# Projection units 3 to 8 of a decoder layer by seven block products

## What is computed

```
proj = x @ w_in                      # x (1032, 1024), w_in (1024, 2568)
u_pool, q, k, v, o_pre, gates = split(proj)      # 512 each, gates 8
y_pool = pool mixer of u_pool;  h = mLSTM(q, k, v, gates), 4 heads of 128
x1 = LayerNorm(alpha*x + concat(y_pool, sigmoid(o_pre)*h) @ w_out)
x2 = LayerNorm(alpha*x1 + square(relu(x1 @ w_ff1 + b1)) @ w_ff2 + b2)
```

## Time and profile before

| | us |
|---|---|
| median of 3 runs | 1094.43 (1094.29 to 1094.94) |
| the profiled execution | 1094.71 |
| its span, first to last instruction | 1091.8 |
| TensorE busy in it | 1071.1 |
| VectorE busy | 662.8 |
| ScalarE busy | 485.2 |

### The profile page before, as it was taken

How to read it: one execution, slowest core, us unless ns; L and a number is a source line. 1 busy time by engine, 2 the same in 40 slices (tenths; PEclk the granted TensorE clock), 3 DMA queues, 4 the chain that set the end, 5 groups by cost and what they waited for, 6 DMA issues and landing times. The chain is left out here.

```text
span 1091.8 us, 19336 instructions
## 1 busy us (share of the span) xinstructions
PE 1071.1 (98%) x8083; PEld 1061.3 (97%) x8083; DVE 662.8 (61%) x901; ACT 485.2 (44%) x690; POOL 99.2 (9%) x122
## 2 busy tenths in 40 slices
PE   8999999999999999999999999999999999999994
PEld 7999999999989999999999999999999999999994
DVE  4512222225588965866555655548767577878966
ACT  4623434343264666655555455456352323334112
POOL 3100000010210321000000000000000000000056
PEclk9999999999999999999999999999999999999998
DMA  9322222233135652143543543568623515335213
GB/s 262 82 76 58 61 58 61 59 90 89 46 118 165 181 182 79 62 137 117 157 153 116 166 143 120 177 205 297 223 91 136 175 59 174 117 92 182 97 41 116
DMA packets 95151, 137.05 MB, mean 126 GB/s; under 512 B 5889, under 2 KB 54753, under 8 KB 94692
## 3 DMA queue, kind: packets, MB, share of 16 engines
q1 hardware_dynamic: 91756, 125.33, 36.4%
q0 software_dynamic: 3328, 10.77, 3.6%
HBM read 101.34 MB, written 34.97 MB: 125 GB/s over the span
## 5 line engine op out<-in xcount | busy, mean ns | idle before, releaser
L1755 PE MATMUL bank<-x_hi,w_hi 128*128 128x344 f32 (+1 forms) x792 | 259.4, 327 | 0.6 <-DVE x_lo L1300 0.6
L1755 PE MATMUL bank<-x_hi,w_lo 128*128 128x344 f32 (+1 forms) x792 | 253.0, 320 | 0.0
L1755 PE MATMUL bank<-x_lo,w_hi 128*128 128x344 f32 (+1 forms) x792 | 252.7, 319 | 0.0
L1755 PE MATMUL bank<-x_hi,d_lo 128*128 128x258 f32 x968 | 222.4, 282 | 0.0
L1755 PEld LDWEIGHTS bank<-x_hi,d_lo 128*128 128x128 f32 x968 | 165.7, 189 | 0.0
L1755 PEld LDWEIGHTS bank<-x_hi,w_hi 128*128 128x128 f32 (+1 forms) x792 | 147.2, 186 | 2.0 <-DVE x_lo L1300 0.9
L1755 PEld LDWEIGHTS bank<-x_lo,w_hi 128*128 128x128 f32 (+1 forms) x792 | 147.0, 186 | 1.1
L1755 PEld LDWEIGHTS bank<-x_hi,w_lo 128*128 128x128 f32 (+1 forms) x792 | 147.0, 186 | 1.1
L1755 PE MATMUL bank<-x_lo,s_hi 128*128 128x258 f32 x448 | 126.5, 282 | 0.0
L1755 PE MATMUL bank<-x_hi,s_hi 128*128 128x258 f32 x448 | 126.4, 282 | 0.0
L1755 PE MATMUL bank<-t_hi,s_hi 128*128 128x258 f32 x336 | 95.2, 283 | 0.2 <-issue 0.2
(11 more groups left out here) (318 smaller groups left out, 2252.2 us busy)
## 6 DMA issues: line engine op xcount, KB each, us to landing
h_ops<-h_unit SPq DMA_DIRECT2D x56, 258.0 KB, 2.5
x_lo_raw<-h_ops SPq DMA_DIRECT2D x14, 1032.0 KB, 5.3
s_raw<-in_w_ff SPq DMA_DIRECT2D x14, 1024.0 KB, 7.0
w_raw<-in_w_out SPq DMA_DIRECT2D x12, 1024.0 KB, 5.6
x_lo_raw<-h_ops SPq DMA_DIRECT2D x14, 774.0 KB, 4.6
...
```

Of the source, the lines that this page charges most:

```text
L1755: return nc.tensor.matmul(out, lhsT, rhs, start=start, stop=stop, skip_group_check=True)
```

## The change

Units 3 to 8 (`by_seven`) compute token blocks 0 and 1 in seven products of half depth (4 chunks, 12 matmuls) instead of eight, as Strassen's scheme in Winograd's form does; block 2 stays as it was, cut in four pieces of 12. With x11, x21 the lower and upper four chunks of block 0, x12, x22 those of block 1, and w11, w12, w21, w22 the same for the two column halves (`quarter`), the sums are

- of x, once for all units: T3 = x22 - x12, T2 = T3 + x11, T4 = x21 - T2, T1 = x12 - x11;
- of weights, in each unit: S1 = w21 + w22, S2 = S1 - w11, S3 = w11 - w21, S4 = w12 - S2.

TensorE's eleven steps in a unit (`seven` on `pe`), with the attention parts between them:

1. w12 by x21, bank 1
2. w11 by x11, bank 0; behind it gap part 0
3. block 2, first half of f 0, bank 3
4. S2 by T2, onto bank 0; behind it part 1
5. S1 by T1, bank 2
6. block 2, second half of f 0, bank 3; part 2
7. S3 by T3, onto bank 0
8. S4 by x22, onto bank 2; part 3
9. block 2, first half of f 1, bank 3
10. w22 by T4, onto bank 0; part 4
11. block 2, second half of f 1, bank 3; part 5

Bank 0 accumulates four of them and ACT copies it after steps 2, 4 and 10; VectorE adds bank 1, bank 0 (after step 7) and bank 2 to the copies (`ps_add`). The high parts of S3, S4, w21, w22 are written over those of S and w that are used up, during the unit (`ps_hi`), and their low parts follow (`ps_lo`). Low parts of raw weights go into the raw slot itself (`RL`), so the next load into that slot waits for the unit's end.

The sums of x are made in unit 2 (`t_sums`, `t_hi_parts`) and live in rows that are free: rows of `Y` for the pooling channels, rows behind `QKV`, the window buffer, the place of `w_pool`, and the third slot of `rows_bc` (now a ring of two). T1 takes the place of x12 in XH and XL; x12 is stored to DRAM before (`b12_d`, two DMAs of 704 KB) and loaded again in unit 8. Unit 2 therefore does block 1 first (`chain_block`). `w_pool` is loaded at the end of unit 8.

```diff
+        def by_seven(u):
+            return SU0 <= u < SU1
...
                 kind, j = PROJ[u - 1]
-                if u >= 2:
+                if u == SU0 - 1:
+                    sp.wait_ge(x_lo, 2 * len(TILES))
+                    for x, t in enumerate((XH, XL)):
+                        sb, dr = block1(t, x)
+                        sp.dma_start(dr, sb).then_inc(b12_out, 16)
+                if by_seven(u - 2):
+                    sp.wait_ge(gemm_done, outputs_to(u - 2))
+                elif u >= 2:
                     sp.wait_ge(lo_done, u - 1)
...
-                if u >= 4:
-                    load_rows(u - 4)
+                if u >= 3:
+                    load_rows(u - 3)
+                if u == SU1:
+                    sp.wait_ge(b12_out, 48)
+                    sp.wait_ge(ps_done, NPP * (SU1 - 1 - SU0) + 5)
+                    for x, t in enumerate((XH, XL)):
+                        sb, dr = block1(t, x)
+                        sp.dma_start(sb, dr).then_inc(b12_in, 16)
...
+            def ps_sums(v):
+                dve.wait_ge(raw_in[v % 2], RAW_AT[v])
+                dve.wait_ge(gemm_done, outputs_to(v - 2))
+                V.tensor_tensor(S1, w21, w22, ALU.add).then_inc(ps_sum, 1)
+                dve.wait_ge(ps_sum, n(4, 1))
+                V.tensor_tensor(S2, S1, w11, ALU.subtract).then_inc(ps_sum, 1)
+                V.tensor_tensor(S3, w11, w21, ALU.subtract).then_inc(ps_sum, 1)
+                dve.wait_ge(ps_sum, n(4, 2))
+                V.tensor_tensor(S4, w12, S2, ALU.subtract).then_inc(ps_sum, 1)
...
+            def seven(u, part):
+                part(0)
+                ps_add(u, 1, 0, 0, 2, 1, bank[1])
+                ps_lo_sum(u, 2, 3, 0)
+                part(1)
+                ps_lo_sum(u, 3, 2, 2)
+                ps_lo_raw(u, 4, 2, 3)
+                part(2)
+                ps_lo_raw(u, 5, 3, 1)
+                prep_lo(u, 2)
+                ps_add(u, 2, 1, 1, 6, 3, bank[0])
+                part(3)
+                ps_add(u, 3, 0, 1, 7, 2, bank[2])
+                prep_lo(u, 3)
+                part(4)
+                prep_lo(u, 4)
+                part(5)
...
+                elif i == 4:
+                    dve.wait_ge(gemm_done, N_GATE + 6 * (SU0 - 2) + 4)
+                    dve.wait_ge(b12_out, 48)
+                    t1 = XLS[:, 0:4, blk(1)]
+                    t_step(t1, x_at(1, 0, 1), x_at(1, 0, 0), ALU.subtract)
+                    t_step(t1, t1, x_at(0, 0, 1), ALU.add)
+                    t_step(t1, t1, x_at(0, 0, 0), ALU.subtract)
...
+                pe.wait_ge(ps_lo, n(5, 3))
+                pe.wait_ge(gemm_read, n0 + 3)
+                product(2, hi(2), sum_lo(2), x_of(1, 1), False, True).then_inc(ps_done, 1)
+                part(3)
+                pe.wait_ge(ps_lo, n(5, 4))
+                pe.wait_ge(gemm_read, n0 + 4)
+                product(3, hi(3), raw_lo(2), x_of(0, 2), True, False)
+                pe.wait_ge(ps_lo, n(5, 5))
+                pe.wait_ge(ps_added, n(3, 2))
+                product(0, hi(1), raw_lo(3), t_of(4), False, True).then_inc(ps_done, 1)
+                part(4)
+                product(3, hi(1), raw_lo(3), x_of(1, 2), False, True).then_inc(gemm_done, 5)
+                part(5)
```

More of the change, by code:

```diff
@@ L781, in divide, with ps_hi_12, ps_hi_34, ps_out @@
                         .then_inc(hn_ready, 1)
+            def ps_hi_12(v):
+                act.wait_ge(raw_in[v % 2], RAW_AT[v])
+                act.wait_ge(gemm_done, outputs_to(v - 2))
+                A(by_k(place(WH, v, 0, 2)), wslot(RAW, v)[:, :, 0:P], ACT.Copy).then_inc(ps_hi, 1)
+            def ps_hi_34(v):
+                act.wait_ge(ps_sum, at_su(v)(4, 2))
+                A(place(WH, v, 2, 2), place(WS, v, 0, 2), ACT.Copy).then_inc(hi_done, 1)
+            def ps_out(u, f, b):
+                kind, j = PROJ[u - 1]
+                if kind == "B" and f:
+                    return Y[:, 4 + j, blk(b)]
+                return QKV[j % 2][:, f if kind == "A" else 2, blk(b)]
@@ L783, in _ @@
             for u in range(1, U_OUT):
-                if u > 1:
+                if u > 1 and prep_gap(u) is None:
                     split_hi(u + 1)
@@ new lines, in ps_add @@
+            def ps_add(u, c, f, b, product, copied, src):
+                kind, j = PROJ[u - 1]
+                dve.wait_ge(ps_done, at_su(u)(NPP, product))
+                dve.wait_ge(gemm_read, N_GATE + 6 * (u - 1) + copied)
+                if kind == "B" and f:
+                    y = Y[:, 4 + j, blk(b)]
+                else:
+                    y = QKV[j % 2][:, f if kind == "A" else 2, blk(b)]
+                stt(y, src[:, 0:BLK], DH ** -0.5 if kind == "A" and f else 1.0, y, ALU.mult, ALU.add).then_inc(ps_added, 1)
@@ L1287, in _ @@
                         (att1, att2, att3)[part](p)
+                if by_seven(u):
+                    seven(u, att_part)
+                    continue
+                for i in range(6):
+                    att_part(i)
+                    if u > 1:
+                        prep_lo(u, i)
+                    if u == SU0 - 1 and i:
+                        t_sums(i)
                     if u >= 9 and i in (3, 5):
@@ L1868, in att3, with seven, product, part @@
                 last.then_inc(num_ready, 1)
+            def seven(u):
+                n, n0 = at_su(u), N_GATE + 6 * (u - 1)
+                first = u == SU0
+                hi = lambda x: lambda k: place(WH, u, x)[:, P * k:P * (k + 1)]
+                sum_lo = lambda x: lambda k: place(WL, u, x)[:, P * k:P * (k + 1)]
+                raw_lo = lambda x: lambda k: wslot(RL, u)[:, 4 * (x % 2) + k, P * (x // 2):P * (x // 2 + 1)]
+                x_of = lambda half, b: (lambda k: XH[:, 4 * half + k, blk(b)], lambda k: XL[:, 4 * half + k, blk(b)])
+                t_of = lambda x: (lambda k: t_at(x, False, k), lambda k: t_at(x, True, k))
+                def product(b, w_hi, w_lo, xs, start, stop):
+                    for k in range(4):
+                        o = bank[b][:, 0:BLK]
+                        mm(o, w_hi(k), xs[0](k), start and k == 0, False)
+                        mm(o, w_hi(k), xs[1](k), False, False)
+                        last = mm(o, w_lo(k), xs[0](k), False, stop and k == 3)
+                    return last
+                def part(i):
+                    x, p = gap_pair(u, i)
+                    if x is not None:
+                        (att1, att2, att3)[x](p)
+                pe.wait_ge(ps_lo, n(5, 1))
+                if first:
+                    pe.wait_ge(gemm_read, n0 - 1)
+                product(1, hi(1), raw_lo(1), x_of(1, 0), True, True).then_inc(ps_done, 1)
+                pe.wait_ge(gemm_read, n0 - 1)
+                product(0, hi(0), raw_lo(0), x_of(0, 0), True, False).then_inc(ps_done, 1)
+                if not first:
+                    pe.wait_ge(ps_added, n(3, 0))
+                part(0)
+                pe.wait_ge(gemm_read, n0)
+                product(3, hi(0), raw_lo(0), x_of(0, 2), True, False).then_inc(ps_done, 1)
+                pe.wait_ge(lo_done, u + 1)
+                pe.wait_ge(gemm_read, n0 + 1)
+                if first:
+                    pe.wait_ge(tx_lo, T_LO0 + 2)
+                product(0, hi(2), sum_lo(0), t_of(2), False, False).then_inc(ps_done, 1)
+                part(1)
+                if first:
+                    pe.wait_ge(tx_lo, T_LO0 + N_THI[1] - T_HI0)
+                product(2, hi(3), sum_lo(1), x_of(0, 1), True, False).then_inc(ps_done, 1)
+                product(3, hi(1), raw_lo(1), x_of(1, 2), False, True).then_inc(gemm_done, 1)
+                part(2)
+                pe.wait_ge(ps_lo, n(5, 2))
+                pe.wait_ge(gemm_read, n0 + 2)
+                product(0, hi(0), sum_lo(3), t_of(3), False, False).then_inc(ps_done, 1)
+                pe.wait_ge(ps_lo, n(5, 3))
+                pe.wait_ge(gemm_read, n0 + 3)
+                product(2, hi(2), sum_lo(2), x_of(1, 1), False, True).then_inc(ps_done, 1)
+                part(3)
+                pe.wait_ge(ps_lo, n(5, 4))
[4 more added lines that the diff above has]
+                product(0, hi(1), raw_lo(3), t_of(4), False, True).then_inc(ps_done, 1)
+                part(4)
+                product(3, hi(1), raw_lo(3), x_of(1, 2), False, True).then_inc(gemm_done, 5)
+                part(5)
```

265 lines of the change are left out of this document (228 added, 37 removed).

## The result

| | before | after |
|---|---|---|
| median | 1094.94 us (1094.29 to 1095.3, 5 runs) | 1083.59 us (1083.06 to 1083.77, 5 runs) |
| the profiled execution, its span | 1094.71, 1091.8 | 1083.06, 1081.0 |
| TensorE, VectorE busy | 1071.1, 662.8 | 1059.1, 723.0 |

The ratio is 0.9896, 95% interval 0.9885 to 0.9907: faster by 1%. The forecast was 1083.9 us. The medians are 11.35 us apart, the spans of the profiled executions 10.8. What lies outside the span was 2.9 us in the profiled execution before and 2.1 in the one after (2.1 to 2.2 in all five after). What follows goes by spans and rows of the traces.

The account below looks back on a forecast made before the run. TensorE, busy 98% of the span, was taken to bound the kernel, so fewer matmuls save time: -11.3 (matmuls) + 1.5 (entry to unit 3) - 0.7 (start) = -10.5 us, forecast 1083.9 us, range 1082 to 1089.5.

Parts of the forecast that it names:

- Matmuls removed: Units 3 to 8 on TensorE: 72 fewer 344-column matmuls at 0.157 us each, 11.3 us less.
- No wait in a steady unit: Projection units after the entry: every bank copy and low part ready in time, 0 us, bounds 0 and 1 us a unit.
- Rival (a): Small waits of 1 us in each of six units, at bank 0's turn or attention parts: 1090 us, chance 0.12.
- Into unit 3: Entry to unit 3: VectorE's sums of x and ACT's work behind them make TensorE wait, +1.5 us, bounds 0 and 4.
- The half microsecond at bank 0: Unit 3: ACT copies bank 0 only after T1's high part, at 83.5 us where TensorE wants it at 83.0: 0.5 us.
- The wait at att2: Unit 3, second attention part: k_weighted ready at 86.4 us where it was due at 85.4, a wait of 1.0 us.
- Start: First loads: w_pool's load moved away shortens TensorE's waits for tiles of x, -0.7 us, bounds 0 and -2.1.
- Sum: Whole kernel: -11.3 + 1.5 - 0.7 = -10.5 us, giving 1083.9 us against the median of 1094.43.
- My low end of the range: Whole kernel, the forecast's lower bound: -11.3 - 2.1 + 1.0 = -12.4 us, 1082 us.
- (b): Unit 3 entered late, at its bound of 4 us instead of 1.5, with nothing gained at the start: 1087 us, chance 0.10.
- (c): Raw weights of units 5 to 9, issued later, land too late and delay step 10: slower, 1100 us at 20.5, chance 0.03.
- (d): Waits at bank turns let TensorE's clock drop to 1.2 GHz, one in four of 66 products: +31 us, 1115, chance 0.02.

Follow-up runs that it names:

- padded: Changed kernel, S3 computed 2, 5, 7 or 9 times more in units 3 to 7, making VectorE later: 1082.94, 1090.36, 1104.01, 1114.43 us.
- late-issue runs: Changed kernel, raw-weight loads for units 5 to 9 held back until step 5 or step 7 of the unit before has ended: 1085.79 and 1118.23 us.

## Why the prediction was right

**Matmuls removed: right.** 72 fewer at 0.157 us; 1.90 us in the mean found in each steady unit where 1.89 was said, and again 1.89 when two units were put back.

**No wait in a steady unit: right**, with the tightest place named rightly and its margin, 2.1 us, found as 2.3 by making VectorE later until it was gone, and unit 8's, 0.8 said, 0.81 in the trace. Rival (a) falls with that: no wait repeats in the list, and 1.4 us more on VectorE in units 3 to 7 cost nothing. One reading was off without harm: the raw weights are issued 0.6 us ahead of the unit, not 0.1 us into it.

**Into unit 3: right in kind, too dear in size.** +1.5 us was said, 0.96 found. The half microsecond at bank 0 did not come: VectorE was through T1's sums at 80.7, not 81.7, half of it the earlier start, half because instructions that don't wait for each other start 1.50 us apart though each is shown with 1.59 (71.71, 73.21 and 74.71 are such starts). ACT's copy was done at 82.4 for the 83.5 said, and step 4 wanted it at 82.5 for the 83.0 said. The wait at att2 was 0.64 for 1.0, but a wait here costs some 0.24 us more than it shows, which my sum had left out. The estimate of 1.59 us for a 1376-column operation came out (1.58 to 1.59 measured), as did the formula of the Trainium skill ("VectorE: DVE Perf Modes", "The TRN2 errata") that gave the same.

**Start: the right load, half the mechanism, -0.48 for -0.7.** The load was moved alone and gives all of it. But I had it shorten both waits, 1.5 and 0.6 us. The one for the sample tile went, and that is the gain; those for the prompt tiles grew, from 1.5 to 2.4 us. So the sum of the waits, which I said would be shorter, got longer while the end got earlier. That -0.7 lay near -0.48 is in part luck: it was most of a 1.0 us that did not come off the way I had it.

**Sum.** -11.3 + 1.0 - 0.5 = -10.8, the span's difference; said -10.5. The two misses, half a microsecond less cost and a quarter less gain, partly cancel. That the medians agree to 0.3 us (1083.59 for 1083.9) says less than it seems: the sum started from a median of 1094.43, the five runs since have 1094.94, and the forecast carried the 2.9 us outside the span along, of which 2.1 were left. My low end of the range had a slip too: with the bound of 0 for unit 3 it would be -13.4, not -12.4. Nothing turned on it.

**The rivals.** (b) did not occur. (c) is a real bound that this kernel keeps more than 10 us away from (weights land 6.3 us after their issue in the median, the issue is 0.6 us ahead of the unit, and the limit is 17.2), and it would have turned the sign earlier than I said. (d) I weighed against a page: "A second HAM failure mode: psum-queue depth-cycling" in the Trainium skill's "TensorE: Matmul & The Clock Gate" has banks cycled and micro-idles between groups behind a swinging clock. Here eleven bank turns a unit left it at 1.00, and so did waits up to 1.5 us, and two of 1.6 and 1.9 us for a tile of x at the start of the padded and the late-issue runs; waits of 2.7 to 2.9 us brought it down in four units of five, those of 4.1 us and more in all. So in this kernel it is long waits, not the turns, on which the clock hangs. Between 1.9 and 2.67 us no run looked.
